# Attention's product with v in plain fp32, in one layer of a hybrid encoder on one Trainium2 core

## What is computed

```python
def block(args):
    ...
    s = jnp.einsum('bqhmd,bkhmd->bhmqk', qi, k).astype(jnp.float32) * scale + bias
    pr = jax.nn.softmax(s, axis=-1)
    a = pr[:, :, 0] - lam * pr[:, :, 1]
    return jnp.einsum('bhqk,bkhe->bqhe', a.astype(v.dtype), v)
```

## Time and profile before

| | |
|---|---|
| median of 3 runs | 3187.45 us |
| the profiled execution's own time | 3191.59 us |
| its span | 3190.1 us |
| mean granted TensorE clock in it | 0.919 |
| PE busy | 2760.1 us, 87% of the span |
| DVE busy | 1641.2 us, 51% |
| ACT busy | 1309.3 us, 41% |
| POOL busy | 284.7 us, 9% |

### The profile page before, as it was taken

The page is one execution under the profiler, slowest core; times in us unless marked ns, Lnnn a source line. Parts: engine busy times, 40 slices in busy tenths (PEclk is TensorE's granted clock), DMA queues, the critical chain, the costliest instruction groups (busy, mean ns, idle before and its releaser), DMA issues. The chain is left out here.

```text
span 3190.1 us, 41940 instructions
## 1 busy us (share of the span) xinstructions
PE 2760.1 (87%) x15536; PEld 2364.5 (74%) x15536; DVE 1641.2 (51%) x2216; ACT 1309.3 (41%) x1848; POOL 284.7 (9%) x323
## 2 busy tenths in 40 slices
PE   3999999796667679688797796589999999999798
PEld 2789888585555447577586685589999999999687
DVE  5100000261788687540564225767777777777555
ACT  4111111151566664431443212245555555555445
POOL 1000000000000100020111001101011010110112
PEclk6999999898798799889799897589999999999899
DMA  8422211274230234473974764178788787887442
GB/s 280 104 81 67 99 66 61 80 240 132 80 88 11 69 112 130 142 237 116 310 250 155 226 197 167 55 229 252 239 247 259 242 248 236 247 259 239 137 174 93
DMA packets 451003, 530.92 MB, mean 166 GB/s; under 512 B 18680, under 2 KB 387208, under 8 KB 449896
## 3 DMA queue, kind: packets, MB, share of 16 engines
q1 hardware_dynamic: 421232, 412.91, 41.4%
q0 software_dynamic: 29664, 116.57, 11.6%
HBM read 401.30 MB, written 128.12 MB: 166 GB/s over the span
## 5 line engine op out<-in xcount | busy, mean ns | idle before, releaser
L2128 DVE TENSOR_TENSOR ex_w_lo<-ex_w_raw,ex_w_hi 128x2048 fp32r<-128x2048 f32 x195 | 443.9, 2291 | 143.0 <-ACT ex_w_hi L2085 143.0
L2217 PE MATMUL ex_ps_u<-ex_x,ex_w_hi 128*128 128x384 f32 x2048 | 411.7, 341 | 5.1 <-DVE ex_w_lo L2128 5.1
L2085 ACT ACTIVATE ex_w_hi<-ex_w_raw 128x2048 fp32r<-128x2048 f32 x195 | 370.4, 1908 | 0.8
L2217 PEld LDWEIGHTS ex_ps_u<-ex_x,ex_w_hi 128*128 128x128 f32 x2048 | 349.1, 189 | 6.1 <-issue 5.5
L2217 PEld LDWEIGHTS ex_ps_u<-ex_x,ex_w_lo 128*128 128x128 f32 x2048 | 266.2, 192 | 0.6
L2217 PE MATMUL ex_ps_u<-ex_x,ex_w_lo 128*128 128x192 f32 x2048 | 266.0, 273 | 0.0
L2236 PE MATMUL ex_ps_d<-ex_w_hi,ex_h 128*128 128x512 f32 x768 | 265.8, 400 | 0.0
L354 DVE TENSOR_TENSOR w_lo<-w_raw,w_hi 128x2048 fp32r<-128x2048 f32 x15 | 34.3, 2289 | 404.4 <-ACT w_hi L322 404.4
L328 ACT ACTIVATE stage<-ps 128x512 f32<-128x512 f32 (+1 forms) x102 | 55.8, 547 | 415.0 <-PE ps L376 359.6
L2236 PE MATMUL ex_ps_d<-ex_w_lo,ex_h 128*128 128x512 f32 x512 | 202.9, 396 | 0.0
L2236 PEld LDWEIGHTS ex_ps_d<-ex_w_hi,ex_h 128*128 128x128 f32 x768 | 144.6, 188 | 35.0
(11 more groups left out here) (385 smaller groups left out, 5221.7 us busy)
## 6 DMA issues: line engine op xcount, KB each, us to landing
ex_w_raw<-in_w_exp_gate SPq DMA_DIRECT2D x64, 1024.0 KB, 5.2
ex_w_raw<-in_w_exp_up SPq DMA_DIRECT2D x64, 1024.0 KB, 6.1
ex_w_raw<-in_w_exp_down SPq DMA_DIRECT2D x64, 1024.0 KB, 6.7
w_raw<-in_w_in SPq DMA_DIRECT2D x15, 1024.0 KB, 5.5
mg_w_raw<-in_w_ssm_up SPq DMA_DIRECT2D x24, 512.0 KB, 5.4
mg_g_raw<-g_d SPq DMA_DIRECT2D x24, 512.0 KB, 7.3
xbcT_d<-stage POOLq DMA_DIRECT2D x5, 1536.0 KB, 5.6
cv_raw<-xbcT_d POOLq DMA_DIRECT2D x10, 768.0 KB, 5.7
```

The lines of the kernel that those rows point to most:

```text
L2085: act.activation(w_hi[:, j % CUT], w_raw[:, j % RAW], ACT.Copy).then_inc(w_hi_done, 1)
L2128: dve.tensor_tensor(w_lo[:, j % CUT], w_raw[:, j % RAW], w_hi[:, j % CUT].bitcast(F32), ALU.subtract).then_inc(w_split, 1)
L2217: last = pe.matmul(ps_u[:, j % 2, m, 0:wide * C], w[:, s, k, cols], x[:, k, 0:wide].rearrange("p a c -> p (a c)"), start=i == 0, stop=i == ...
```

## The change

The product with v is made of plain fp32 matmuls. Five things go with it:

- VectorE copies the turned map from PSUM into one tile `aT` in fp32 (a copy at the place of L809). ScalarE's copy `aT_hi` and the tile `aT_lo` are gone. The copy waits for `turned`, and for `pv_full` of two units earlier.
- v is not split: ScalarE's copy L763 and VectorE's remainder L804 are gone, and SyncE loads v straight into its double-buffered tile. For heads 2 and 3 it waits for `pv_full` first, until the products of the head two earlier are done; v's load, and the bias behind it, stand after that wait.
- For each 128 keys there is one fp32 matmul of 128 columns in place of the wide and the narrow one.
- A unit has one output tile. ScalarE's copy `beside` is gone.
- GpSimd's sum is gone; GpSimd stores each head when ScalarE's copies of it are counted.

The diff, cut to its core:

```diff
@@ tiles
-        raw, v_raw = sb("raw", [P, 2, T]), sb("v_raw", [P, TT, P])
+        raw = sb("raw", [P, 2, T])
-        v = sb("v", [P, 2, TT, 2, P], F32R)
+        v = sb("v", [P, 2, TT, P])
-        aT_hi, aT_lo = sb("aT_hi", [P, 2, T1], F32R), sb("aT_lo", [P, 2, T1], F32R)
-        o, beside = sb("o", [P, 2, TT, P]), sb("beside", [P, 2, P])
+        aT = sb("aT", [P, 2, T1])
+        o = sb("o", [P, 2, TT, P])
@@ SyncE
-                sp.dma_start(v_raw[:], v_in[:, :, head * VD:(head + 1) * VD]).then_inc(landed, 16)
+                if head >= 2:
+                    sp.wait_ge(pv_full, PER * (head - 1))
+                sp.dma_start(v[:, hs], v_in[:, :, head * VD:(head + 1) * VD]).then_inc(landed, 16)
@@ GpSimd
-            for j, (head, g0, b, L) in enumerate(UNITS):
-                pool.wait_ge(o_copied, j + 1)
-                tile = o[:, head % 2, g0 // P + b]
-                pool.tensor_tensor(tile, tile, beside[:, j % 2], ALU.add).then_inc(o_added, 1)
-                if (j + 1) % PER == 0:
-                    store(head)
+            for head in range(HEADS):
+                pool.wait_ge(o_copied, PER * (head + 1))
+                pool.dma_start(o_out[:, :, head * P:(head + 1) * P], o[:, head % 2]).then_inc(o_stored[head % 2], 16)
@@ ScalarE
-                    act.activation(k_hi[:, hs], raw[:, 1], ACT.Copy)
-                    act.activation(v[:, hs, :, 0], v_raw[:], ACT.Copy).then_inc(hi_split, 1)
+                    act.activation(k_hi[:, hs], raw[:, 1], ACT.Copy).then_inc(hi_split, 1)
-                if 2 <= k < NU + 2:
-                    j = k - 2
-                    L = UNITS[j][3]
-                    act.wait_ge(turned, j + 1)
-                    if j >= 2:
-                        act.wait_ge(pv_full, j - 1)
-                    act.activation(aT_hi[:, j % 2, 0:L], ps_t[:, 0:L], ACT.Copy).then_inc(hi_done, 1)
-                    if j >= 2:
-                        act.wait_ge(o_added, j - 1)
-                    act.activation(o[:, head % 2, g0 // P + b], ps_o[:, j % 2, 0:P], ACT.Copy, scale=whole)
-                    act.activation(beside[:, j % 2], ps_o[:, j % 2, P:2 * P], ACT.Copy, scale=whole).then_inc(o_copied, 1)
+                    act.activation(o[:, head % 2, g0 // P + b], ps_o[:, j % 2, 0:P], ACT.Copy, scale=whole).then_inc(o_copied, 1)
@@ VectorE
-                    dve.tensor_tensor(k_lo[:, hs], raw[:, 1], k_hi[:, hs].bitcast(F32), ALU.subtract)
-                    dve.tensor_tensor(v[:, hs, :, 1], v_raw[:], v[:, hs, :, 0].bitcast(F32), ALU.subtract).then_inc(lo_split, 1)
+                    dve.tensor_tensor(k_lo[:, hs], raw[:, 1], k_hi[:, hs].bitcast(F32), ALU.subtract).then_inc(lo_split, 1)
-                    dve.wait_ge(hi_done, j + 1)
-                    dve.tensor_tensor(aT_lo[:, j % 2, 0:L], ps_t[:, 0:L], aT_hi[:, j % 2, 0:L].bitcast(F32), ALU.subtract).then_inc(lo_done, 1)
+                    dve.wait_ge(turned, j + 1)
+                    if j >= 2:
+                        dve.wait_ge(pv_full, j - 1)
+                    dve.tensor_copy(aT[:, j % 2, 0:L], ps_t[:, 0:L]).then_inc(aT_done, 1)
@@ TensorE
-                        both = v[:, head % 2, g0 // P + c]
-                        wide = (ps_o[:, j % 2, 0:2 * P], aT_hi[:, j % 2, c * P:(c + 1) * P], both.rearrange("p a e -> p (a e)"))
-                        narrow = (ps_o[:, j % 2, 0:P], aT_lo[:, j % 2, c * P:(c + 1) * P], both[:, 0])
-                        for product in ((wide, narrow) if c == 0 else (narrow, wide)):
-                            last = pe.matmul(*product, start=c == 0 and product is wide, stop=c == L // P - 1 and product is wide)
+                        last = pe.matmul(ps_o[:, j % 2, 0:P], aT[:, j % 2, c * P:(c + 1) * P], v[:, head % 2, g0 // P + c], start=c == 0, stop=c == L // P - 1)
```

More of the change, by code:

```diff
@@ L711, in attend @@
         inverted, weighed, mixed = sem("inverted"), sem("weighed"), sem("mixed")
-        turned, hi_done, lo_done = sem("turned"), sem("hi_done"), sem("lo_done")
-        pv_full, o_copied, o_added = sem("pv_full"), sem("o_copied"), sem("o_added")
+        turned, aT_done = sem("turned"), sem("aT_done")
+        pv_full, o_copied = sem("pv_full"), sem("o_copied")
         block = ctx.enter_context(nc.Block())
@@ L735, in _ @@
         def _(pool):
-            def store(head):
-                pool.wait_ge(o_added, PER * (head + 1))
+            for head in range(HEADS):
+                pool.wait_ge(o_copied, PER * (head + 1))
                 pool.dma_start(o_out[:, :, head * P:(head + 1) * P], o[:, head % 2]).then_inc(o_stored[head % 2], 16)
-            for j, (head, g0, b, L) in enumerate(UNITS):
-                pool.wait_ge(o_copied, j + 1)
-                tile = o[:, head % 2, g0 // P + b]
-                pool.tensor_tensor(tile, tile, beside[:, j % 2], ALU.add).then_inc(o_added, 1)
-                if (j + 1) % PER == 0:
-                    store(head)
             for done in o_stored:
@@ L858, in _ @@
                     if j:
-                        pe.wait_ge(lo_done, j)
+                        pe.wait_ge(aT_done, j)
                     for c in range(L // P):
@@ L865, in _ @@
                     head, g0, b, L = UNITS[j]
-                    pe.wait_ge(lo_done, j + 1)
+                    pe.wait_ge(aT_done, j + 1)
                     if j >= 2:
```

## The result

The changed kernel takes **3142.76 us** (median of 4 runs, 3141.01 to 3144.38), the kernel before on the same chip 3188.25 us (4 runs, 3186.66 to 3189.99): a ratio of 0.9857, 95% interval 0.984 to 0.9874, or 45.5 us less. The forecast was 28.4 us less, 3159, with 3147 as the fast end of the range.

What follows compares the result with a forecast made beforehand. No engine is full in the attention stage, so waits decide, VectorE's above all. Terms 11.6 + 12.5 + 3.1 + 1.2 = 28.4 us off 3191.6 give 3163.2, run median 3159; bounds 3150 to 3168, stated range 3147 to 3173.

Steps and rivals of the forecast that it cites:

- the steady term: Attention's steady units: VectorE's wait for ScalarE's map copy goes, less 6.3 us lost to scores; 11.6 us gained, 8 to 18.
- the feared loss: Steady units: in 14 iterations an earlier copy only lengthens VectorE's wait for scores; 14 x 0.45 = 6.3 us lost.
- The splits at heads 1 to 3: Later splits: ScalarE's copies and its remainder of v go, 4.2 us each, three times; 12.5 us gained.
- The first split: First head's split, with no map ahead of it: 1.4 + 1.67 = 3.1 us gained.
- The copy: VectorE's copy of the turned map from PSUM, 1024 columns: priced at the subtraction's 1.23 us.
- The prediction's rival: VectorE's PSUM copy runs at double rate, about 0.7 us, and TensorE takes over: 3150 us; chance 0.04.
- The product: TensorE's plain fp32 product with v, eight matmuls of 128 columns: taken as 1.88 us, against 2.02 before.
- v was late nowhere: v's transfer, held for heads 2 and 3, counted as nothing: lands in time with 2.3 us to spare.
- The tail: End of the attention stage: aT_hi, beside and GpSimd's sum go; 1.2 us gained, between 0.8 and 1.8.
- TensorE did not become the bound: Rival in the attention units: new product takes 2.7 us, TensorE becomes the bound, 14 us lost: 3173; chance 0.08.
- The slower rival: Attention stage: plain fp32 work leaves TensorE's clock low, 2.9 us per further long unit, up to 3247 us; chance 0.06.
- the third and the first rival: Third: VectorE's copy at double rate, 3150, chance 0.04. First: v lands late at heads 2 and 3, 3168, chance 0.12.

Runs made afterwards that it cites:

- experiment 11: The kernel before, unchanged, run once more for a second profile: 3188.93 us (one run).
- Experiment 5: The kernel of experiment 1 plus six extra unread TensorE products at each head's first short unit: 3165.82 us.
- experiment 3: The changed kernel with ScalarE copying a still tile at the old copy's place, nobody waiting for it: 3147.52 us.
- experiment 4: The changed kernel with v's split work kept on ScalarE and VectorE, into tiles nobody reads: 3154.68 us.
- experiment 6: The changed kernel with every second matmul of the product with v left out: 3145.20 us (one run).
- experiment 10: The kernel before plus six extra unread TensorE products at each head's first short unit: 3187.68 us.
- experiment 12: Changed kernel with map copy on ScalarE, v awaited separately and loaded behind the bias, plus unread TensorE products in long idle stretches: 3119.64 us.
- experiment 1: The changed kernel with the old wait put back: VectorE's copy waits for a ScalarE copy nobody reads: 3170.22 us.

## Why the prediction was off

**The step that failed** is the steady term, 11.6 us. It took 6.3 us off for waits for scores: "in the other 14 iterations an earlier copy only lengthens the wait for scores". The first two, the three behind-split and the 39 plain intervals together gave 1.9 + 2.1 + 25.5 = 29.5 (22.7 against the profile of experiment 11). Even the term's upper bound, 18, was no more than the length of the wait itself, 17.9. Two things were wrong.

First, the waits for scores were taken as independent of the wait that goes, when more than half of them, 8.1 of 15.3 us, came with a fallen clock. These are six of the 14, one at each first short unit and two in head 3; windows of five microseconds there have a granted clock of 0.60 to 0.68 in the profile of before. Five stand behind an idle stretch of TensorE of 1.88 or 1.92 us, the sixth behind several of 0.92 us at most. Experiment 5 gives the share: with the clock held up at the short units and the old wait in place, the plain intervals take 187.30, less 0.73 for one long unit of 6.46 at which the clock fell even so, so 186.6 us. To 170.40 are 16.2 us for the wait itself; ScalarE's load has no part in them (170.41 in experiment 3). In the first two intervals and behind the splits there are five long units more, at 0.59 each 2.9: 19.1. From 195.85 to 186.6 are 9.3 us for the falls of the clock in that execution, 4.7 in that of experiment 11. The two, 19.1 and 9.3, make 28.4 of the 29.5; the last 1.1 are not split further. Against experiment 11's profile 19.1 and 4.7 make 23.8, 1.1 more than its 22.7. That 28.4 is also the forecast's whole sum is chance.

Second, the wait itself came back whole, 19.1 us of 17.9 counted. The short units do keep new waits for scores, 0.8 us a head (0.44, 0.17, 0.20 in head 0), which is what became of the feared loss. They are outweighed by a gain I had not seen: a copy that waits for nothing starts some 0.08 us before the mix ahead of it ends, so that a long unit is 5.14, not 5.23.

**What held.** The splits at heads 1 to 3: 45.56 - 33.20 = 12.4 us, 12.5 forecast; experiments 3 and 4 split each into 3.05 us for v and 0.95 for ScalarE's copies, near the working's 1.4 + 1.67 and 0.9 + 0.25. The first split: 34.35 - 31.39 = 3.0, 3.1 forecast. The copy: 1.22 us, forecast 1.23, at no double rate. The prediction's rival took "up to 2x" from the perf-mode tier table of the Trainium skill (VectorE: DVE Perf Modes), which is for PSUM operands of any type; below it, under "Why PSUM operands drop a tier", the same page leaves fp32 from PSUM at 1x. This case's trace agrees, 1.22 us for the copy as for the subtraction before it. The product: 1.88 us, as taken. v was late nowhere but at the start (ScalarE waits for it once, 7.3 us). The tail gave 2.7 instead of 1.2: VectorE's last wait there was 1.9 us for ScalarE and is now 0.8 for TensorE, and I had taken that one to be held by the product anyway.

**The rivals.** TensorE did not become the bound (experiment 6). The product's eight matmuls of 128 columns take 1.88 us, 0.235 each, as long as one matmul of 512 columns in the next stage (0.23). The rule of four passes for true FP32 in the Trainium skill (FP8 and Floating Point Precision, TensorE Precision Notes) agrees with that. What the rival drew from it does not follow: the old pair was no cheaper, and half of the product gone changes nothing in a long unit. The slower rival was about the right quantity with the wrong sign. The clock had a part, and it rose: 0.82 to 0.90 in the stage. The one remark against that rival, that TensorE's idle time shrinks here, was the step to follow through. Behind an idle stretch of 1.97 us the granted clock was 0.66, and experiment 5 took both away. The Trainium skill (TensorE: Matmul & The Clock Gate, "A second HAM failure mode") describes a kernel that lost throughput because TensorE idled briefly and often between groups of matmuls and its clock went to and fro; this case's trace agrees.

**The range.** The written bounds, 8 to 18 and 0.8 to 1.8, reach from 3152 to 3163 only; 3150 and 3168 are the times of the third and the first rival. Even both fast ends together leave 3142.8 out.

**Left open**: why the clock fell after 11 of 12 like idle stretches and not after the twelfth, why only after 6 of 18 that were hardly shorter, and whether extra products at one place bring falls at another (experiment 10).

## What to carry to other kernels

A wait on the engine that sets the pace can be worth more than its own length where TensorE idles meanwhile and comes back at a lower clock (19.1 us for the wait, 4.7 to 9.3 more for the clock here): read the granted clock window by window, and ask of each later wait whether it follows from the one that goes, before taking it off the gain. When an idle stretch of TensorE stands just ahead of work on the path, products that nobody reads can pay for themselves (9.7 us in experiment 12), but only the time tells: the same trick in the kernel before shortened four units and not the run.

## What the runs showed of the hardware

- Idle stretches of TensorE of about 1.9 us between two groups of matmuls were often followed by a lower granted clock, though not always. Over the next five microseconds it was 0.64 to 0.66 behind 11 of 12 stretches of 1.92 to 1.98 us at a head's first short unit, where a product took 3.43 us instead of 1.88 (experiment 1); 0.62 to 0.66 behind 6 of 18 stretches of 1.87 to 1.90 us at a head's second unit; and 1.00 behind all 14 stretches of 1.65 to 1.73 us. After 0.33 us (changed kernel) or 0.45 (experiment 5) at the first short unit it stayed at 1.00.
- The lower level is not only an affair of the first matmuls: in the kernel before the stage averages 0.82, and with TensorE kept busy it is 1.00 from 785 to 1015 us of a stage that runs from 773 to 1025 (experiment 12).
- A VectorE instruction that waits for nothing starts about 0.08 us before the one ahead of it ends (copies of 1.22 us stand 1.13 from the next instruction), so removing a wait gives that too.
- A plain fp32 matmul is two instructions; with 128 columns the pair takes 0.235 us at the full clock, no dearer than the wide and narrow pair that it replaced (0.25).
